# Expert rows weighed on the way out of PSUM and summed in DRAM by an adding scatter

## The chip, the cores and the metric

One core of a Trainium2 chip runs the kernel. The metric is device time in microseconds (us), as the median of several runs of the same program. The kernel before takes 1257.65 us (three runs, 1256.83 to 1258.01). Five engines work beside one another on the core: TensorE (PE, matrix products), VectorE (DVE), ScalarE (ACT), GpSimd (POOL) and SyncE (SP, which only issues transfers). Sixteen DMA engines move data between DRAM and the on-chip memory (SBUF); matrix products land in PSUM, which has eight banks of 128 x 512 fp32.

## The reference, cut to what matters

A transformer-like encoder layer for 1536 tokens of width 1024, in fp32. The first half (adaLN, spatial gating, pooling, output projection, layer norm) is not touched except that some work is put beside it. The second half is a mixture of 32 experts with two experts per token:

```python
g_w  = softmax(g_logits)[g_idx]                       # top-1 group
e_w  = softmax(top2(e_logits in group)) * g_w         # two weights per token
for each block of 128 rows of one expert:             # rows sorted by expert
    xb = h_pad[tok]
    gu = xb @ w_gate_up[e]
    y  = (silu(gu[:, :512]) * gu[:, 512:]) @ w_down[e]
    out[tok] += y * w[:, None]
x = layer_norm(ALPHA * x + g2 * out, ln2_g, ln2_b)
```

So there are 3072 pairs of token and expert. For the last layer norm each token needs the weighted sum of its two expert rows.

## The kernel before, in words

Activations and weights are split into a high and a low fp32r part, and each product is made of three fp32r matmuls (`three`: high by high, high by low, low by high). ACT makes the high parts, DVE the low ones.

**The expert loop.** The router's result is a list of 39 blocks of 128 rows, each of one expert. Block i runs through all engines, each of which has its own in-order queue:

- POOL: `gather(i)` copies the block's column of row numbers into `g_idx` and gathers 128 rows of 4 KB into `xg`; `scatter(i)` copies the column of `table_s` into `s_idx`, waits for `y_ready` and scatters the block's result `y_sb` into `y_rows`. In one pass of POOL's loop `gather(i + 2)` stands ahead of `scatter(i - 1)`. Row numbers past the bound are left out, so that only real rows are written. `y_rows` has 3072 rows, one for each pair.
- PE: `gate_up(i)`, transposes of the next `xg`, `down(i - 1)`, transposes of the activations (`a_transposes_e`).
- ACT (`expert_block`): three high parts of the next expert's gate and up weights (`high_gu`), `silu`, `high_xT`, the fourth `high_gu`, two `high_dn`, `take_y(i - 1)` (copies the result of `down` from PSUM banks 5 and 6 to `y_sb`, L1035), `high_aT(i)` (L1020). The weight work is done only where the expert changes.
- DVE: the low parts in the same order (`low_gu` L1514, `gate` L1524, `low_xT`, `low_dn` L1518, `low_aT` L1528).
- SP: loads of 1 MB each into seven slots for gate and up weights and four for down weights (L611, L619); a load is released when PE has used its slot.

**The end.** SP reads layer-1 rows into `fin` (L674) and the last constants (L682), waits until all scatters have landed, and then reads for each of the 12 token tiles the two rows of each token, `y0` and `y1` (L690, L691). PE forms the weighted sum with matmuls against diagonal matrices of weights (`diag`, L2086 and L2087). The last block is not scattered: its rows are weighed, kept in SBUF (`last_h`, `last_l`) and added by two matmuls with a one-hot matrix (L2090, L2091). To find its rows and weights there is a chain of small DVE and PE operations (L1595 to L1613, L2069, L2072), and `clear_last` writes zeros to its places in `y_rows` early on. Then for each tile DVE multiplies by the gate (L1624, two halves out of PSUM), adds `ALPHA * x` with a row sum (L1628), ACT makes mean and squares (L1114, L1116), POOL the reciprocal deviation (L820, L822), DVE subtracts the mean and multiplies by the gain (L1631) and makes the final scale and bias (L1636). For two of the 12 tiles (`PE_TILES`) the final scale is two matmuls per half on PE (L2097 with the bias row, L2098 with a diagonal of deviations) and ACT copies the result from PSUM (L1108) and stores it.

## Time and profile before

| | before |
|---|---|
| median of three runs | 1257.65 us |
| the profiled execution's own time | 1256.84 us |
| its span (first to last instruction) | 1255.1 us |
| mean granted clock of TensorE | 0.989 |
| busy: PE, DVE, ACT, POOL | 1221.6, 905.0, 614.6, 216.6 us |
| DMA | 329.21 MB, mean 262 GB/s |
| start of the expert loop's first silu | 479.4 us, then 38 equal blocks of 17.68 us but for the first (16.35) |
| last `take_y` of the loop | 1172.71 us |

"Span" is what the trace covers; the device time is 1.7 us more. The table's shares are averages over stages with different limits, so a change is read from its own stage. Times within the trace count from the start of the span. An instruction's row gives its start, how long it took, the engine, the line of the kernel, the operation and the tiles (out<-in); in square brackets stands how long the engine sat idle before it and who ended that.

### The profile page before, as it was taken

To read this page: it belongs to the slowest core of one execution; us is meant where nothing else is said; L and a number is where in the kernel's file an instruction comes from. 1 tells how busy PE (TensorE), PEld (TensorE's weight loads), DVE (VectorE), ACT (ScalarE), POOL (GpSimd) and SP (SyncE) were. 2 spreads that over 40 slices of the span, in tenths; PEclk is the share of its full clock that TensorE was granted. 3 is DMA by queue.
4 is the path that set the end of the run, shared out by engine and by line. 5 is a ranking of instruction groups with operands and counts; after the bars stand their busy time and mean duration, and the time that the engine had idled before them with its cause. 6 is when DMAs were issued, how large, how long until landed. Compare 5 with 4: busy or idle time off the path is not lost.

```text
span 1255.1 us, 25398 instructions
## 1 busy us (share of the span) xinstructions
PE 1221.6 (97%) x7491; PEld 1005.2 (80%) x7492; DVE 905.0 (72%) x1138; ACT 614.6 (49%) x681; POOL 216.6 (17%) x282
## 2 busy tenths in 40 slices
PE   6999999999999998999999999999999999999897
PEld 5889999998888855888888888888888888888553
DVE  3546345657999988856887566745889888998497
ACT  3331111131222244547775565645777877787523
POOL 0042311000111111111121111111121221222122
PEclk8999999999999999999999999999999999999998
DMA  9944311035333588767998766955999999998994
GB/s 312 303 135 133 120 51 35 18 135 184 120 116 128 207 308 305 293 257 283 373 400 348 262 261 246 345 219 214 377 402 403 396 400 397 389 395 305 337 407 170
DMA packets 122711, 329.21 MB, mean 262 GB/s; under 512 B 12888, under 2 KB 44704, under 8 KB 122660
## 3 DMA queue, kind: packets, MB, share of 16 engines
q1 hardware_dynamic: 107700, 288.08, 61.5%
q0 software_dynamic: 13088, 34.13, 7.6%
q10 hardware_dynamic: 1872, 6.29, 1.3%
q8 instruction: 35, 0.57, 0.2%
q14 instruction: 16, 0.13, 0.0%
HBM read 296.97 MB, written 39.39 MB: 268 GB/s over the span
## 4 chain that ended last, share of the span: by engine, by line
PE 79%; DVE 10%; issue 3%; DMA 3%; SPq 2%; POOL 2%; ACT 1%; POOLq 0%; DVEq 0%; ACTq 0%
PE bank L1660 19%; PE bank L1662 19%; PE bank L1661 19%; PE bank L1673 4%; PE bank L1675 4%; PE bank L1674 3%; PE bank L1991 3%; POOL rstd L756 2%; PE bank L2086 1%; PE bank L2087 1%; PE bank L2015 1%; DVE h L1378 1%; DMA sh2b<-mod_rows 1%; PE bank L1720 1%; PE bank L1729 1%
## 5 line engine op out<-in xcount | busy, mean ns | idle before, releaser
L1514 DVE TENSOR_TENSOR gu_l<-gu_raw,gu_h (+1 forms) x128 | 287.3, 2287 | 39.4 <-ACT gu_h L1006 25.4
L1660 PE MATMUL bank<-gu_h,xT_h 128*128 (+1 forms) x624 | 247.2, 396 | 1.8 <-DVE xT_l L1533 1.5
L1006 ACT ACTIVATE gu_h<-gu_raw (+1 forms) x128 | 239.0, 1927 | 9.9 <-issue 7.1
L1662 PE MATMUL bank<-gu_h,xT_l 128*128 (+1 forms) x624 | 243.8, 391 | 0.0
L1661 PE MATMUL bank<-gu_l,xT_h 128*128 (+1 forms) x624 | 243.4, 390 | 0.0
L1518 DVE TENSOR_TENSOR dn_l<-dn_raw,dn_h (+1 forms) x64 | 143.6, 2286 | 7.3 <-ACT dn_h L1010 3.9
L1660 PEld LDWEIGHTS bank<-gu_h,xT_h 128*128 128x128 f32 x624 | 117.6, 188 | 25.3 <-issue 2.2
L1662 PEld LDWEIGHTS bank<-gu_h,xT_l 128*128 128x128 f32 x624 | 117.5, 188 | 25.0
L1661 PEld LDWEIGHTS bank<-gu_l,xT_h 128*128 128x128 f32 x624 | 117.7, 189 | 23.3
L1660 PE MATMUL bank<-dn_h,aT_h 128*128 (+1 forms) x308 | 123.2, 400 | 0.0
L1662 PE MATMUL bank<-dn_h,aT_l 128*128 (+1 forms) x308 | 120.1, 390 | 0.0
L1661 PE MATMUL bank<-dn_l,aT_h 128*128 (+1 forms) x308 | 120.0, 390 | 0.0
L1673 PE MATMUL bank<-hT_h,win_h 128*128 128x256 f32 x384 | 111.3, 290 | 8.3 <-DVE hT_l L1192 7.2
L1010 ACT ACTIVATE dn_h<-dn_raw (+1 forms) x64 | 119.0, 1912 | 0.6 <-issue 0.6
L1675 PE MATMUL bank<-hT_h,win_l 128*128 128x256 f32 x384 | 108.4, 282 | 0.0
L1016 ACT ACTIVATE act_s<-bank 128x512 f32<-128x512 f32 x39 | 23.3, 598 | 173.6 <-PE bank L1662 173.6
L1674 PE MATMUL bank<-hT_l,win_h 128*128 128x256 f32 x384 | 108.3, 282 | 0.0
L793 POOL DMA_INDIRECT y_rows<-y_sb,s_idx x38 | 70.5, 1856 | 186.6 <-ACT y_sb L1035 181.0
L1673 PEld LDWEIGHTS bank<-hT_h,win_h 128*128 128x128 f32 x384 | 73.4, 191 | 10.6 <-DVE hT_l L1192 7.5
L1524 DVE TENSOR_TENSOR act_s<-bank,act_s 128x512 f32<-128x512 f32 x39 | 27.0, 692 | 75.2 <-ACT act_s L1016 75.2
L1660 PE MATMUL bank<-wout_h,z_h 128*128 128x512 f32 x192 | 78.2, 407 | 0.0
L1662 PE MATMUL bank<-wout_h,z_l 128*128 128x512 f32 x192 | 75.9, 395 | 0.0
(312 smaller groups left out, 2037.6 us busy)
## 6 DMA issues: line engine op xcount, KB each, us to landing
gu_raw<-in_w_gate_up SPq DMA_DIRECT2D x128, 1024.0 KB, 8.8
dn_raw<-in_w_down SPq DMA_DIRECT2D x64, 1024.0 KB, 8.2
y<-y_rows SPq DMA_DIRECT2D x22, 512.0 KB, 8.4
ada_raw<-in_w_ada SPq DMA_DIRECT2D x20, 512.0 KB, 7.2
ada_raw<-in_w_ada SPq DMA_DIRECT2D x10, 1024.0 KB, 5.6
win_raw<-in_w_in SPq DMA_DIRECT2D x8, 768.0 KB, 9.0
h_rows<-h SPq DMA_DIRECT2D x12, 512.0 KB, 2.7
fin<-x_rows SPq DMA_DIRECT2D x12, 512.0 KB, 11.3
```

The source lines that it names most:

```text
L793: nc.gpsimd.indirect_dma_start(out=y_d, out_offset=bass.IndirectOffsetOnAxis(ap=s_idx[:, 0:1], axis=0), in_=y_sb[:], in_offset=None, bound ...
L1006: nc.scalar.activation(gu_slot(gu_h, e, c), gu_slot(gu_raw, e, c), ACT.Copy).then_inc(S["gu_split_h"], 1)
L1010: nc.scalar.activation(dn_slot(dn_h, e, c), dn_slot(dn_raw, e, c), ACT.Copy).then_inc(S["dn_split_h"], 1)
L1514: nv.tensor_tensor(gu_slot(gu_l, e, c), gu_slot(gu_raw, e, c), gu_slot(gu_h, e, c).bitcast(F32), ALU.subtract).then_inc(S["gu_split_l"], 1)
L1518: nv.tensor_tensor(dn_slot(dn_l, e, c), dn_slot(dn_raw, e, c), dn_slot(dn_h, e, c).bitcast(F32), ALU.subtract).then_inc(S["dn_split_l"], 1)
L1660: mm(out, lh, rh, start=start, stop=False)
L1661: mm(out, lh, rl, start=False, stop=False)
L1662: return mm(out, ll, rh, start=False, stop=stop)
L1673: mm(out, win_h[:, k, c], hT_h[s][:, k, :], start=start, stop=False)
L1674: mm(out, win_h[:, k, c], hT_l[s][:, k, :], start=False, stop=False)
L1675: return mm(out, win_l[:, k, c], hT_h[s][:, k, :], start=False, stop=stop)
L1991: last = nc.tensor.transpose(ps[2 + k // 4][:, (k % 4) * P:(k % 4 + 1) * P], xg[:, k * P:(k + 1) * P], ident[:])
```

## The change

- **Weights.** The two weights of each token are made in the loop's first block instead of the second, and ACT writes them to DRAM (`w_rows`, 3072 numbers). For each block POOL now gathers its 128 weights into `w_slot`, by indices from `table_s`. `take_y` multiplies by `w_slot` as it copies, so it now waits for that gather, and for the scatter before.
- **Sum.** `y_rows` has one row per token. The scatter adds in DRAM (`compute_op=ALU.add`), by token numbers from a second table, `table_t`. Each scatter waits until the one before has landed. `y_rows` is cleared beforehand by 12 transfers that ACT issues in the mixer stage (`clear_y`).
- **The last block** goes the same way as the others: gather of weights, `take_y`, scatter. The small chains, `diag`, `onehot`, `last_h` and `last_l` and their matmuls are gone.
- **End.** SP loads all 12 `fin` tiles at once, and one `y` tile per token tile. DVE multiplies it by the gate in SBUF in one instruction. Ten tiles instead of two get their final scale on PE.

```diff
-PE_TILES = (NT - 4, NT - 3)
+PE_TILES = tuple(range(NT - 2))
+W_ROWS = T
...
-        y_d = nc.dram_tensor("y_rows", (PAIRS, D), F32).ap()
+        y_d = nc.dram_tensor("y_rows", (T, D), F32).ap()
+        w_d = nc.dram_tensor("w_rows", (2 * W_ROWS, 1), F32).ap()
...
-            for t in range(6):
+            for t in range(NT):
                 load_x1(t)
...
                 if t >= F_SLOTS:
-                    sp.wait_ge(S["y_summed"], 2 * (t - F_SLOTS + 1))
-                for part in ((slice(0, 512), slice(512, D)) if t == 0 else (slice(0, D),)):
-                    sp.dma_start(y0[s][:, part], y_d[bass.ds(t * P, P), part]).then_inc(...)
-                    sp.dma_start(y1[s][:, part], y_d[bass.ds(T + t * P, P), part]).then_inc(...)
+                    sp.wait_ge(S["f_taken"], t - F_SLOTS + 1)
+                sp.dma_start(ys[s][:], y_d[bass.ds(t * P, P), :]).then_inc(y_loaded[s], 16)
...
             def scatter(i):
-                pool.wait_ge(S["y_scattered"], 16 * i + 16)
-                nc.gpsimd.tensor_copy(s_idx[:], table_s[:, bass.ds(column(i), 1)]).then_inc(S["y_idx"], 1)
-                pool.wait_ge(S["y_idx"], i + 1)
+                if not (isinstance(i, int) and i == 0):
+                    pool.wait_ge(S["y_scattered"], 16 * i)
+                col = column(i)
+                nc.gpsimd.tensor_copy(s_idx[:], table_s[:, bass.ds(col, 1)]).then_inc(S["y_idx"], 1)
+                nc.gpsimd.tensor_copy(t_idx[:], table_t[:, bass.ds(col, 1)]).then_inc(S["y_idx"], 1)
+                pool.wait_ge(S["y_idx"], 2 * i + 2)
+                pool.wait_ge(S["y_ready"], i + 1)
+                pool.sem_inc(S["pool_carrier"], 1)
+                nc.gpsimd.indirect_dma_start(out=w_slot[:], out_offset=None, in_=w_d, in_offset=bass.IndirectOffsetOnAxis(ap=s_idx[:, 0:1], axis=0),
+                                             bounds_check=W_ROWS + T - 1, oob_is_err=False).then_inc(S["w_loaded"], 16)
                 pool.wait_ge(S["y_ready"], i + 2)
                 pool.sem_inc(S["pool_carrier"], 1)
-                nc.gpsimd.indirect_dma_start(out=y_d, out_offset=bass.IndirectOffsetOnAxis(ap=s_idx[:, 0:1], axis=0),
-                                             in_=y_sb[:], in_offset=None, bounds_check=PAIRS - 1,
-                                             oob_is_err=False).then_inc(S["y_scattered"], 16)
+                nc.gpsimd.indirect_dma_start(out=y_d, out_offset=bass.IndirectOffsetOnAxis(ap=t_idx[:, 0:1], axis=0),
+                                             in_=y_sb[:], in_offset=None, bounds_check=T - 1,
+                                             oob_is_err=False, compute_op=ALU.add).then_inc(S["y_scattered"], 16)
...
             with pool.Fori(2, n_blocks) as i:
                 gather(i + 2)
                 scatter(i - 1)
-            nc.gpsimd.iota(iota_t[:], pattern=[[1, T]], base=0, channel_multiplier=0, ...)
+            scatter(last_block)
...
+            def clear_y(i):
+                if i == 1:
+                    act.wait_ge(S["lT_zeroed"], 1)
+                for t in range(3 * (i - 1), 3 * i):
+                    nc.scalar.dma_start(y_d[t * P:(t + 1) * P, :].rearrange("p (a n) -> p a n", n=P), lT[:, None, :].to_broadcast([P, D // P, P])).then_inc(S["y_cleared"], 16)
...
             def take_y(i):
                 act.wait_ge(S["dn_used"], 2 * i + 2)
-                act.wait_ge(S["y_scattered"], 16 * i + 16)
+                act.wait_ge(S["w_loaded"], 16 * i + 16)
+                if not (isinstance(i, int) and i == 0):
+                    act.wait_ge(S["y_scattered"], 16 * i)
                 for b in range(2):
-                    last = nc.scalar.activation(y_sb[:, 512 * b:512 * (b + 1)], ps[5 + b][:], ACT.Copy)
+                    last = nc.scalar.activation(y_sb[:, 512 * b:512 * (b + 1)], ps[5 + b][:], ACT.Copy, scale=w_slot[:, 0:1])
                 last.then_inc(S["y_ready"], 1)
...
+                    act.wait_ge(S["tab_ready"], 2)
+                    for c in range(2):
+                        nc.scalar.dma_start(..., out=w_d[c * W_ROWS:c * W_ROWS + T, :].rearrange("(t p) o -> p (t o)", p=P), in_=wts[:, c, :]).then_inc(S["w_stored"], 16)
...
-            act.wait_ge(S["tab_ready"], 3)
-            for t in range(NT):
-                for c in range(2):
-                    last = nc.scalar.activation(diag[:, c, t, :], ident[:], ACT.Copy, scale=wts[:, c, t:t + 1])
...
+            take_y(last_block)
...
             def f_residual(t):
-                for b in range(2):
-                    dve.wait_ge(S["y_summed"], 2 * t + b + 1)
-                    c = slice(512 * b, 512 * (b + 1))
-                    last = nv.tensor_tensor(gated[:, c], ps[bank + b][:], g2b[q][:, c], ALU.mult)
-                last.then_inc(S["f_gated"], 1)
+                q, y = 0 if t < SEQ_TILES[0][1] else 1, ys[t % F_SLOTS]
+                dve.wait_ge(y_loaded[t % F_SLOTS], 16 * (t // F_SLOTS + 1))
+                nv.tensor_tensor(y[:], y[:], g2b[q][:], ALU.mult).then_inc(S["f_gated"], 1)
...
             down_last()
+            down(last_block, NE - 1, (1,))
             pe.wait_ge(S["list_dve"], 5)
-            nc.tensor.transpose(ps[7][:, 0:P], row_sel[:], ident[:]).then_inc(S["list_pe"], 1)
-            down(last_block, NE - 1, (1,))
...
-                    mm(ps[bank + b][:], diag[:, 0, t, :], y0[slot][:, n], start=True, stop=False)
-                    mm(ps[bank + b][:], diag[:, 1, t, :], y1[slot][:, n], start=False, stop=False)
...
             for i, t in enumerate(PE_TILES):
                 pe.wait_ge(S["f_diag"], i + 1)
                 pe.wait_ge(S["f_gained"], t + 1)
+                if i >= F_BANKS:
+                    pe.wait_ge(S["f_copied"], 2 * (i - F_BANKS) + 2)
```

How the instructions stand on POOL, from the end of the loop's body on (L772 and L775 are `gather`, `ISA` rows are register work), before:

```order
82 L772 COPY g_idx<-table_g 128x1
84 L775 DMA xg<-h_rows,g_idx 128x1024
90 L789 COPY s_idx<-table_s 128x1
92 L793 DMA y_rows<-y_sb,s_idx 3072x1024
95 L812 IOTA iota_t 128x1536
```

and now, where L752 and L755 are the same `gather`:

```order
79 L752 COPY g_idx<-table_g 128x1
81 L755 DMA xg<-h_rows,g_idx 128x1024
87 L762 COPY s_idx<-table_s 128x1
89 L763 COPY t_idx<-table_t 128x1
91 L767 DMA w_slot<-w_rows,s_idx 128x1
93 L771 DMA y_rows<-y_sb,t_idx 1536x1024
101 L762 COPY s_idx<-table_s 128x1
103 L763 COPY t_idx<-table_t 128x1
106 L767 DMA w_slot<-w_rows,s_idx 128x1
108 L771 DMA y_rows<-y_sb,t_idx 1536x1024
```

The gather of weights has come between the gather of rows and the scatter, on the same queue, and the whole sequence stands once more behind the loop for the last block.

On DVE, one token tile at the end (of tile 5 and the steps of the tiles before it that run with it), before:

```order
651 L1624 TENSOR_TENSOR gated<-bank,g2b_217 128x512 x2
652 L1628 SCALAR_TENSOR_TENSOR fin_199,f_sum<-fin_199,gated 128x1024
653 L1631 SCALAR_TENSOR_TENSOR fin_198<-fin_198,f_mean,ln_gb 128x1024
654 L1636 SCALAR_TENSOR_TENSOR fin_197<-fin_197,f_rstd,ln_bb 128x1024
```

and now:

```order
627 L1582 TENSOR_TENSOR y_208<-y_208,g2b_214 128x1024
628 L1585 SCALAR_TENSOR_TENSOR fin_200,f_sum<-fin_200,y_208 128x1024
629 L1588 SCALAR_TENSOR_TENSOR fin_199<-fin_199,f_mean,ln_gb 128x1024
```

Three instructions a tile are left of five; the fifth, the final scale, has gone to PE for ten tiles. On PE what stands behind the last down projection was, for one half tile, four matmuls of the sum:

```order
2462 L2086 MATMUL bank<-y_3_209,diag 128x512
2463 L2087 MATMUL bank<-y_3_213,diag 128x512
2464 L2090 MATMUL bank<-last_h,onehot 128x512
2465 L2091 MATMUL bank<-last_l,onehot 128x512
2466 L2097 MATMUL bank<-ln_bb,ones_row 128x512
2467 L2098 MATMUL bank<-fin_202,diag_r 128x512
```

and is now the final scale alone, 20 times two matmuls:

```order
2367 L1619 MATMUL bank<-dn_h,aT_l 128x512
2368 L2034 MATMUL bank<-ln_bb,ones_row 128x512
2369 L2035 MATMUL bank<-fin_196,diag_r 128x512
2370 L2034 MATMUL bank<-ln_bb,ones_row 128x512
2371 L2035 MATMUL bank<-fin_196,diag_r 128x512
```

## Rows read from the trace of the kernel before

**Rows 1.** Windows: stretch, length; busy us of PE, PEld, DVE, ACT, POOL; clock; DMA; GB/s.

```profile
100.00:200.00 100.00, 100.00 (x1173) 92.70 (x1172) 47.63 (x120) 15.76 (x28) 28.28 (x36) 1.00 0.31 96
1000.00:1100.00 100.00, 100.00 (x477) 83.39 (x476) 89.20 (x59) 77.69 (x68) 21.13 (x24) 1.00 1.01 396
```

**Rows 2.** The page: GB/s in 40 slices of 31.4 us.

```profile
GB/s 312 303 135 133 120 51 35 18 135 184 120 116 128 207 308 305 293 257 283 373 400 348 262 261 246 345 219 214 377 402 403 396 400 397 389 395 305 337 407 170
```

**Rows 3.** Timeline of ACT in a block late in the loop, then two blocks on.

```profile
1095.57 0.60 ACT L1016 ACTIVATE act_s<-bank 128x512 f32<-128x512 f32 x1 [3.44 <-PE bank L1662]
1097.42 1.92 ACT L1006 ACTIVATE gu_h<-gu_raw  x1
1102.82 1.09 ACT L1035 ACTIVATE y_sb<-bank 128x512 f32<-128x512 f32 x2
1104.26 5.55 ACT L1006 ACTIVATE gu_h<-gu_raw  x3
1113.25 0.60 ACT L1016 ACTIVATE act_s<-bank 128x512 f32<-128x512 f32 x1 [3.44 <-PE bank L1662]
...
1148.61 0.60 ACT L1016 ACTIVATE act_s<-bank 128x512 f32<-128x512 f32 x1 [3.33 <-PE bank L1662]
...
1150.71 1.92 ACT L1006 ACTIVATE gu_h<-gu_raw  x1
```

**Rows 4.** Timeline of DVE in the same block.

```profile
1101.78 4.49 DVE L1518 TENSOR_TENSOR dn_l<-dn_raw,dn_h  x2
...
1106.79 6.69 DVE L1514 TENSOR_TENSOR gu_l<-gu_raw,gu_h  x3
1113.88 0.69 DVE L1524 TENSOR_TENSOR act_s<-bank,act_s 128x512 f32<-128x512 f32 x1 [0.41 <-ACT act_s L1016]
```

**Rows 5.** Timeline of POOL in the same block.

```profile
1098.27 0.99 POOL L775 DMA_INDIRECT xg<-h_rows,g_idx  x1 [0.83 <-POOL g_idx L772]
1099.26 0.20 POOL L789 COPY s_idx<-table_s 128x1 int32 x1
1104.77 2.36 POOL L793 DMA_INDIRECT y_rows<-y_sb,s_idx  x1 [5.31 <-ACT y_sb L1035]
```

**Rows 6.** Line L793, the scatter: issue to landing.

```profile
DMA to landing us min/median/max: 3.2/8.1/10.8
```

**Rows 7.** DMA queue of POOL: packets, MB, share of 16 engines.

```profile
q0 software_dynamic: 13088, 34.13, 7.6%
```

**Rows 8.** Chain of waits at the end: start, us, what.

```profile
1172.71 0.39 ACT y_sb L1035
...
1175.80 3.99 DMA y_rows<-y_sb,s_idx
1179.80 0.33 SPq L690
```

**Rows 9.** Line L690, the load of y0: issue to landing.

```profile
DMA to landing us min/median/max: 3.0/6.6/9.1
```

**Rows 10.** Timeline of DVE at the end: three starts of the gate.

```profile
1232.65 1.28 DVE L1624 TENSOR_TENSOR gated<-bank,g2b 128x512 f32<-128x512 f32 x2
...
1237.52 1.28 DVE L1624 TENSOR_TENSOR gated<-bank,g2b 128x512 f32<-128x512 f32 x2
...
1241.18 1.28 DVE L1624 TENSOR_TENSOR gated<-bank,g2b 128x512 f32<-128x512 f32 x2
```

**Rows 11.** Timeline of PE at the end: the two tiles scaled there.

```profile
1238.35 1.12 PE L2097 MATMUL bank<-ln_bb,ones_row 1*128 1x512 f32 x2
...
1242.56 1.12 PE L2097 MATMUL bank<-ln_bb,ones_row 1*128 1x512 f32 x2
```

**Rows 12.** Timeline of ACT at the end: squares of the last tile.

```profile
1244.00 1.15 ACT L1116 ACTIVATE squares<-fin,f_mean 128x1024 f32<-128x1024 f32 x1
```

**Rows 13.** Windows, columns as in rows 1: the clock after PE's pauses.

```profile
15.00:20.00 5.00, 3.32 (x14) 3.23 (x15) 2.21 (x4) 3.04 (x6) 0.00 (x0) 0.55 1.11 331
20.00:25.00 5.00, 4.73 (x82) 3.92 (x80) 1.76 (x1) 0.52 (x2) 0.00 (x0) 0.77 1.04 391
...
1248.00:1250.00 2.00, 0.00 (x0) 0.00 (x0) 1.37 (x2) 0.00 (x0) 0.00 (x0) 0.50 0.85 342
```

More of the change, by code:

```diff
@@ L337, in encoder @@
             assert r.at == at + 24 * KB
[L338 to L343 removed]
+        ys = [Region(W0 + 4 * s * KB).take(f"y_{s}", [P, D]) for s in range(F_SLOTS)]
+        r = Region(W0 + 8 * GU_SLOTS * KB + 4 * KB)
         squares = r.take("squares", [P, D])
@@ L1574, in expert_block @@
                     low_gu(e_next, 3)
-                if second:
+                if first:
                     weights()
-                if first:
                     for c in range(2):
```

112 lines of the change are left out of this document (19 added, 93 removed).

## The prediction, made before the changed kernel ran

> **What bounds the kernel now.** I read the windows first. In the mixer stage PE is busy all the time and the DMA engines a third of it; in the late expert loop PE is busy all the time too, at full clock, and beside it the DMA engines stand at a share of 1.01 and 396 GB/s [rows 1]. The page's slices show that this is no single spot: from the 29th to the 36th, 8 slices of 31.4 us = 251 us or 14 blocks of 17.68 us, they read 377 to 403 GB/s [rows 2]. So PE sets the pace of the loop, and DMA is right behind it. How near, ACT tells: the fourth high part of a block needs a 1 MB load that has just come, and starts 1.85 us after the silu in one block (1095.57 to 1097.42) and 2.10 us three blocks on (1148.61 to 1150.71) [rows 3]. The loads slip slowly against PE already. Between them ACT sits idle 3.44 us a block, ahead of the silu, and DVE 0.41 us ahead of the gate [rows 3, 4]. That idle time is all the give there is.
>
> Behind the loop the chain of waits goes from `take_y` (1172.71) to the scatter (issued 1175.80, landed 3.99 later) to SP's loads of y (1179.80) [rows 8], and then with DVE: a tile takes 1237.52 - 1232.65 = 4.87 us there, and 1241.18 - 1237.52 = 3.66 us where the final scale is left to PE [rows 10].
>
> **The end, step by step.** All times count from the start of the span.
>
> (a) `take_y` of the block before the last now waits for its weights. Their gather is issued behind the gather of rows: that one starts 1098.27 in rows 5 when the silu is at 1095.57, the copy of indices follows, one more copy of 0.20 and the pause of 0.83 that stands ahead of an indirect transfer come on top, so it starts some 4.9 us after the silu [rows 3, 5]. Such a block's silu is at 1166.3 (1148.61 + 17.68), which gives 1171.2. From issue to landing the nearest rows are the scatter's: 3.2 at least, 8.1 in the median, 10.8 at most [rows 6]; it could also be under 3.2, since 512 bytes are moved rather than 512 KB. In the same moments SP now has twelve `fin` loads of 512 KB in flight instead of six, and the rows' gather stands ahead in the same queue. I take 7 us, between the least and the median but nearer the latter: 1178.2, that is 5.5 us later than `take_y` starts today. Ends: 1.7 and 9.3 us. Everything behind follows, the last down projection too, since `high_aT` stands behind `take_y` on ACT.
> By the Trainium skill (DMA: Bandwidth & Descriptors, "Anatomy of one DMA — SWDGE (gpsimd) path") a transfer from POOL takes 2.0 us plus its bytes at 436 GB/s. With it the wait would be 0.5 us instead of 5.5. No row here shows a transfer so small that far ahead of its queue, so it is no term of my sum.
>
> (b) `take_y` 1.1 us [rows 3], then the scatter: 1175.80 is 2.0 us after 1173.8, the end of today's `take_y` [rows 3, 8]. It starts at 1181.3. It lands 4.0 us later when it only writes [rows 8]; adding needs the old row as well, and I give it 1 us more (0 to 4): 1186.3.
>
> (c) Only then does POOL copy the last block's indices and gather its weights: two copies of 0.20 and the pause of 0.83 [rows 5], then 3.2 us, the least landing [rows 6], as traffic is over by then: 1190.7. PE's last down projection is done by then. `take_y` 1.1, the step to the scatter 2.0, landing 5.0: 1198.8. Before, this whole second round did not exist, because the last block stayed in SBUF.
>
> (d) SP issues, and the first y tile lands after 3.0 us, the least landing of such a load [rows 9]: DVE starts at 1202.1.
>
> (e) DVE needs per tile 3.6 to 3.66 us [rows 10]: its gate out of SBUF lies between half of a 2048-wide one (6.69 / 3 / 2 = 1.1 us, rows 4) and the two halves of today (1.28). But PE needs more: the two tiles that it scales today start 4.21 us apart, back to back (1238.35 and 1242.56) [rows 11]. Ten tiles make 42.1 us, and PE is the slowest of the three. It starts when tile 0's diagonal is made, which on ACT stands behind tile 1's squares: four DVE instructions of about 1.2 us, then 2 us of ACT: 7.0 us after DVE. By then PE has done nothing for some 20 us. Its clock is at 0.50, that is at 1.2 GHz, already 2 us after PE has stopped at the end, and after the pause at the start it was 0.55 for 5 us and 0.77 for another 5 [rows 13]. The clock lost there is 0.45 x 5 + 0.23 x 5 = 3.4 us, and as PE is the slowest, it is all paid. ACT's last squares come after the copies of tile 8: 7.0 + 9 x 4.21 + 3.4 + 1.3 = 49.6 us after DVE's start, and from their start to the span's end there are 1255.1 - 1244.0 = 11.1 us today [rows 12]. The span would end at 1202.1 + 60.7 = 1262.8: **7.7 us later** than today. The saving of DVE's 4.87 us per tile, of 24 diagonals on ACT and of half of the y traffic is real, but it is spent on the second round of (c), on (a) and on a PE at 4.21 us.
>
> **The loop.** (f) The adding scatter reads each row that it adds to. POOL's queue carries 34.13 MB at 7.6% of the span [rows 7]; 41 gathers of 0.52 MB are 21.5 of it, so the scatters are 12.6 MB. At 7.6% x 1255 / 34.13 = 2.8 us per MB a second reading costs 35 us of all DMA engines, 0.9 us per block. The gather of weights, 128 packets, I put at 0.1: 1.0 us per block, bounds 0 (where the reading hides under the other direction's traffic) and 2.7 (three times the plain price). In the 14 saturated blocks the loads come 14 us later in all. ACT takes up 3.44 of idle, and as PE has the down projection between a silu and the next `gate_up`, I give as much again to that: about 7 us pass before PE waits. Left are **7 to 8 us**; with 0.9 x 14 - 7 = 5.6 and with 2.7 x 14 - 7 = 31 at the upper end, 0 at the lower.
> The Trainium skill (Collectives: The Full Stack, "The bandwidth ceiling: the fold count and why AG ≠ RS ≠ AR") says that it is not the adding that costs in a DMA engine but the second source, both being read through one ring, at half the rate. By that rule the second reading can't hide, and rival 1 below falls away; the plain scatters of rows 6 and 7 can't tell.
>
> (g) `take_y` waits for weights in every block. They are issued 4.9 us after the silu and needed at 7.25 (1102.82 - 1095.57) [rows 3]. With (a)'s landing they come 3 to 5 us late. ACT then finishes its three high parts (5.55 us) at about its silu, where it now has 3.44 us [rows 3]; DVE, with 4.49 us of low parts ahead of `low_aT` [rows 4], loses about 2 us and goes on. PE needs neither before the next block but one. Cost 0, cover: those 3.44 us. It is used up if the weights land later than some 12 us after the silu.
>
> (h) Clearing: 6.3 MB in 12 transfers beside a mixer stage with a DMA share of 0.31 and ACT busy 15.76 of 100 us [rows 1]: 0. The weights made one block earlier and stored as 4-byte pieces in a busy queue: 0, at most 3.
>
> Sum: 1255.1 + 7.7 + 8 = 1270.8 of span. The profiled execution took 1.7 us more than its span, and the median of the runs lies 0.8 above that execution: 1273.
>
> **Rivals.**
> 1. *The reading for the sum hides* in the loop: (f) is 0, only the end costs, 1257.65 + 7.7 = 1265. For it: a plain scatter reads SBUF and writes DRAM, so DRAM's side could have room. Against it: a share of 1.01.
> 2. *The recurrence of weights and scatter takes over the loop.* `take_y`, scatter, its landing, the next gather of weights, its landing, the next `take_y`: 1.1 + 0.9 + 8.1 + 1.2 + 3.2 to 8.1 = 14.5 to 19.4 us, against 17.68 [rows 3, 5, 6]. With the landing 1 to 2 us longer for the adding it is over 17.68 in saturated blocks, by 1 to 2 us in each of 14 to 20: 1257.65 + 7.7 + 25 = 1290.
> 3. *The end gains* (the other side): weights are 512 bytes and land ahead of `take_y`, adding costs nothing, and PE's clock holds. Then DVE starts at 1172.7 + 1.1 + 2.0 + 4.0 + 1.2 + 3.2 + 1.1 + 2.0 + 4.0 + 3.3 = 1194.6 and the end comes 57.3 later, at 1251.9: 1254.5, faster by 0.25%. The point from which it decides is (a): each microsecond for which `take_y` waits is lost, and at a wait of 1 us with the rest as here there is no change.
> 4. *Weights cheap but clock cold*: 3 without the clock: 1258, no change.
>
> **How the numbers follow.** Forecast, 0.42: 1273 (own range 1264 to 1283). Rival 1: 0.20. Rival 2: 0.22. Rival 3: 0.08. Rival 4: 0.08. About 0.2% (2.5 us) is what a measurement can tell from no change. Faster 0.09 (rival 3 and a little), same 0.09, slower 0.82. The range runs from 1258 to 1296: it leaves out rival 3 and the far half of rival 2.
>
> **What would show it.** Right: ACT idle ahead of `take_y` in the loop with the gather of weights as releaser; the fourth high part waiting for its load in the late blocks, PE idle there ahead of `gate_up`; landings of the scatter over 8.1 us in the median; two scatters one after the other before the first load of y; L2034 starts 4.21 us apart per two pairs, later ones evenly, the first at a clock near 0.5. Wrong: blocks of 17.68 us to the end with 400 GB/s and no wait of PE, or `take_y` within 1 us of its place today, or DVE without idle time between the tiles of the end.

## The result, and the profile after

| | before | after |
|---|---|---|
| median, runs on the same chip | 1256.83 us (5 runs) | 1393.38 us (5 runs, 1389.23 to 1395.73) |
| ratio, 95% interval | 1 | 1.1081 (1.1065 to 1.1096) |
| span of the profiled execution | 1255.1 us | 1387.5 us |
| up to the first silu of the expert loop | 495.8 us | 495.0 us |
| first to last silu (38 intervals) | 670.5 us | 760.3 us |
| last silu to DVE's first tile of the end | 20.5 us | 38.6 us |
| from there to the end of the span | 68.4 us | 93.6 us |

The change made the kernel 10.8% slower, and the time is far outside the range of the prediction (1258 to 1296). The four stages of the table are cut at an instruction of ACT or DVE that both kernels have. Of the 132.4 us that the span grew, 89.8 are in the loop, 18.1 between the loop and the end's first tile, 25.2 in the end, and -0.8 ahead of the loop.

A correction to the table that stands ahead of the prediction: it puts the first silu of the loop at 479.4 us. It starts at 495.78, and the 39th at 1166.29; the 38 intervals between them are 16.35 and 37 times 17.68. The prediction used the 17.68 and not the start, so none of its numbers hangs on it.

The waits of the changed kernel (engine, line and what it writes, releaser: us in total, times, longest) name the largest item:

```profile
ACT y_sb L1025 <- DMA w_slot<-w_rows,s_idx: 254.5, 39, 10.9
POOL y_rows L771 <- ACT y_sb L1025: 214.9, 38, 7.4
DVE aT_l L1512 <- ACT aT_h L1008: 164.8, 32, 8.7
```

`take_y` waits for its 128 weights in every one of the 39 blocks, 6.5 us on average, and DVE then waits for ACT. Issue to landing of the gather of weights (L767), least, median, most:

```profile
DMA to landing us min/median/max: 2.3/5.5/7.6
```

ACT in a late block, where [rows 3] shows 3.44 us of idle time, ahead of the silu:

```profile
1087.71 1.92 ACT L998 ACTIVATE dn_h<-dn_raw  x1
1100.54 1.27 ACT L1025 ACTIVATE y_sb<-bank,w_slot 128x512 f32<-128x512 f32 x2 [10.92 <-DMA w_slot<-w_rows,s_idx]
1101.70 0.60 ACT L1008 ACTIVATE aT_h<-bank 128x512 fp32r<-128x512 f32 x1
1102.31 5.51 ACT L994 ACTIVATE gu_h<-gu_raw  x3
1107.73 0.58 ACT L1004 ACTIVATE act_s<-bank 128x512 f32<-128x512 f32 x1
...
1117.72 1.27 ACT L1025 ACTIVATE y_sb<-bank,w_slot 128x512 f32<-128x512 f32 x2 [3.03 <-DMA w_slot<-w_rows,s_idx]
```

The idle time has gone to `take_y`; the silu follows the high parts with no gap (5.51 us from 1102.31, silu at 1107.73). So it is late because ACT is late, and no longer because PE is. POOL in the same block, against [rows 5]:

```profile
1093.19 2.19 POOL L767 DMA_INDIRECT w_slot<-w_rows,s_idx  x1 [0.88 <-POOL t_idx L763]
1102.69 1.60 POOL L771 DMA_INDIRECT y_rows<-y_sb,t_idx  x1 [7.31 <-ACT y_sb L1025]
1103.74 0.75 POOL L752 COPY g_idx<-table_g 128x1 int32 x1
1105.29 2.34 POOL L755 DMA_INDIRECT xg<-h_rows,g_idx  x1 [0.80 <-POOL g_idx L752]
1108.86 2.33 POOL L762 COPY s_idx<-table_s 128x1 int32 x1 [1.23 <-DMA y_rows<-y_sb,t_idx]
1111.14 0.17 POOL L763 COPY t_idx<-table_t 128x1 int32 x1
1112.20 1.03 POOL L767 DMA_INDIRECT w_slot<-w_rows,s_idx  x1 [0.88 <-POOL t_idx L763]
```

This is a circle: `take_y` 1100.54, scatter 1102.69, landed 1108.86, copies of indices, gather of weights 1112.20, landed and `take_y` 1117.72. It takes 17.2 us here, nearly as long as a block of PE's (17.68), and nothing in it overlaps. It is one of the short rounds: from one `take_y` to the next the 38 rounds take 12.6 to 25.3 us, 19.5 on average. The next round takes 22.95, and in it POOL waits for something else:

```profile
1119.87 1.61 POOL L771 DMA_INDIRECT y_rows<-y_sb,t_idx  x1 [6.65 <-ACT y_sb L1025]
1129.91 0.18 POOL L752 COPY g_idx<-table_g 128x1 int32 x1 [8.43 <-PE bank L1948]
1133.09 2.33 POOL L767 DMA_INDIRECT w_slot<-w_rows,s_idx  x1 [0.88 <-POOL t_idx L763]
```

The gather of rows stands ahead of the gather of weights on POOL, and it may not overwrite `xg` before PE has transposed the rows in it (L1948). So in such a round the circle runs through PE: `take_y`, the operands that ACT and DVE make behind it, PE, the gather of rows, the gather of weights. Of POOL's waits between a scatter and the next gather of weights, this is the larger part:

```profile
POOL g_idx L752 <- PE bank L1948: 162.5, 31, 14.4
POOL s_idx L762 <- DMA y_rows<-y_sb,t_idx: 30.0, 16, 5.2
```

Two of these 31 waits (12.06 and 14.44 us) lie ahead of the first scatter. Copies that took 0.20 us in [rows 5] take up to 2.33, and the issue of a gather 2.34 in place of 0.99.

What the loop lost is not all idle time of PE. First to last silu, before and then after:

```profile
495.80:1166.30 670.50, 668.40 (x3169) 556.55 (x3168) 509.17 (x345) 452.42 (x410) 124.15 (x152) 1.00 0.87 333
495.00:1255.30 760.30, 698.60 (x3170) 571.17 (x3169) 506.45 (x346) 458.32 (x410) 278.57 (x224) 0.96 0.85 297
```

PE was idle for 61.7 us in place of 2.1, and for the same matmuls it was busy 30.2 us longer, at a granted clock of 0.96 in place of 1.00. In e2 and e7, where the circle is broken, the clock is 1.00 and 0.99 and PE is busy 672.9 and 674.5 us: the slower clock came with the waits and went with them.

At the start of the loop POOL stands still for another reason, the stores of the weights as 4-byte pieces:

```profile
513.95 0.96 POOL L755 DMA_INDIRECT xg<-h_rows,g_idx  x1 [0.79 <-POOL g_idx L752]
535.90 0.18 POOL L762 COPY s_idx<-table_s 128x1 int32 x1 [20.98 <-DMA w_rows<-wts]
```

ACT issued these stores from 502.15 on (2.10 us for two); they had landed at 535.9. The first three intervals of the loop take 22.62, 24.80 and 21.94 us, 17.7 more than in the kernel before.

The end: ACT, then windows (columns as in [rows 1]).

```profile
1255.29 0.60 ACT L1004 ACTIVATE act_s<-bank 128x512 f32<-128x512 f32 x1 [9.76 <-PE bank L1619]
...
1269.10 1.27 ACT L1025 ACTIVATE y_sb<-bank,w_slot 128x512 f32<-128x512 f32 x2 [8.11 <-DMA w_slot<-w_rows,s_idx]
1270.26 0.60 ACT L1008 ACTIVATE aT_h<-bank 128x512 fp32r<-128x512 f32 x1
1281.73 1.27 ACT L1025 ACTIVATE y_sb<-bank,w_slot 128x512 f32<-128x512 f32 x2 [10.88 <-DMA w_slot<-w_rows,s_idx]
```

```profile
1310.00:1330.00 20.00, 20.00 (x21) 5.00 (x20) 9.69 (x10) 8.20 (x17) 7.63 (x6) 0.50 0.47 158
1350.00:1370.00 20.00, 20.00 (x21) 4.99 (x20) 8.83 (x10) 8.20 (x17) 7.21 (x6) 0.50 0.20 79
```

Two rounds of gather and scatter stand one after the other, as forecast. But then PE is busy for all of 20 us and its granted clock stays at 0.50, that is 1.2 GHz where 1.00 is 2.4 GHz, to the end. The bias matmuls of two tiles start 8.01 us apart (1304.95, 1312.96, 1320.97 for every second one), in place of the 4.21 of [rows 11].

### The profile page after: what moved, and what is told of

Read it like the earlier page. It is cut to its first block, busy times and chain, and to the rows that moved or that the text cites. A ratio compares the mean times of both kernels' runs of the same rounds, so it can differ in the third digit from the quotient of the medians.

```text
span 1387.5 us, 25445 instructions
## 1 busy us (share of the span) xinstructions
PE 1269.5 (91%) x7408; PEld 1009.3 (73%) x7409; DVE 886.7 (64%) x1105; ACT 625.9 (45%) x681; POOL 390.2 (28%) x359
## 3 DMA queue, kind: packets, MB, share of 16 engines
q0 software_dynamic: 14336, 34.16, 10.0%
## 4 chain that ended last, share of the span: by engine, by line
PE 53%; DMA 15%; DVE 11%; issue 10%; POOL 4%; ACT 3%; SPq 1%; POOLq 1%; ACTq 1%; DVEq 1%
PE bank L1617 11%; PE bank L1618 10%; PE bank L1619 10%; DMA w_slot<-w_rows,s_idx 7%; DMA y_rows<-y_sb,t_idx 4%; PE bank L1630 3%; PE bank L1632 3%; PE bank L1631 3%; PE bank L2035 3%; PE bank L2034 3%; DMA w_rows<-wts 2%; PE bank L1948 2%; ACT gu_h L994 1%; POOL rstd L736 1%; DVE gu_l L1498 1%
## 5 line engine op out<-in xcount | busy, mean ns | idle before, releaser
L1617 PE MATMUL bank<-gu_h,xT_h 128*128 (+1 forms) x624 | 254.8, 408 | 31.7 <-issue 30.2
L1619 PE MATMUL bank<-gu_h,xT_l 128*128 (+1 forms) x624 | 250.5, 401 | 0.0
L1618 PE MATMUL bank<-gu_l,xT_h 128*128 (+1 forms) x624 | 250.0, 401 | 0.0
L1617 PEld LDWEIGHTS bank<-gu_h,xT_h 128*128 128x128 f32 x624 | 121.9, 195 | 62.2 <-issue 37.4
L1025 ACT ACTIVATE y_sb<-bank,w_slot 128x512 f32<-128x512 f32 x78 | 49.4, 685 | 254.5 <-DMA w_slot<-w_rows,s_idx 254.5
L1619 PEld LDWEIGHTS bank<-gu_h,xT_l 128*128 128x128 f32 x624 | 121.4, 194 | 26.6
L1618 PEld LDWEIGHTS bank<-gu_l,xT_h 128*128 128x128 f32 x624 | 121.9, 195 | 25.0
L1512 DVE TENSOR_TENSOR aT_l<-bank,aT_h 128x512 fp32r<-128x512 f32 x39 | 26.9, 690 | 164.9 <-ACT aT_h L1008 164.8
L771 POOL DMA_INDIRECT y_rows<-y_sb,t_idx x39 | 64.6, 1657 | 222.4 <-ACT y_sb L1025 214.9
L752 POOL COPY g_idx<-table_g 128x1 int32 (+1 forms) x41 | 32.5, 793 | 185.3 <-PE bank L1948 162.5
L767 POOL DMA_INDIRECT w_slot<-w_rows,s_idx x39 | 68.7, 1762 | 35.7 <-POOL t_idx L763 32.8
```

Of the source, the lines that this page charges most:

```text
L767: nc.gpsimd.indirect_dma_start(out=w_slot[:], out_offset=None, in_=w_d, in_offset=bass.IndirectOffsetOnAxis(ap=s_idx[:, 0:1], axis=0), bou ...
L771: nc.gpsimd.indirect_dma_start(out=y_d, out_offset=bass.IndirectOffsetOnAxis(ap=t_idx[:, 0:1], axis=0), in_=y_sb[:], in_offset=None, bound ...
L1617: mm(out, lh, rh, start=start, stop=False)
L1618: mm(out, lh, rl, start=False, stop=False)
L1619: return mm(out, ll, rh, start=False, stop=stop)
```

## The experiments

Each kernel's profile is cut at the same places. All rows are from one profiled execution each. "First three" is what the first three intervals take beyond those of before.

| kernel | median us | ratio to before, interval | loop | first three | last silu to DVE | DVE to end |
|---|---|---|---|---|---|---|
| before | 1256.8 | 1 | 670.5 | 0 | 20.5 | 68.4 |
| after | 1393.4 | 1.1081 (1.1065, 1.1096) | 760.3 | 17.7 | 38.6 | 93.6 |
| e1 plain scatter | 1369.0 | 1.0881 (1.0850, 1.0913) | 744.8 | 19.8 | 34.7 | 93.6 |
| e2 no gather of weights | 1312.6 | 1.0433 (1.0403, 1.0464) | 689.7 | 8.3 | 32.5 | 93.6 |
| e3 PE warmed | 1388.8 | 1.1039 (1.0955, 1.1122) | 767.6 | 21.9 | 39.4 | 88.6 |
| e4 whole stores | 1374.4 | 1.0925 (1.0822, 1.1028) | 739.3 | 4.1 | 39.6 | 93.6 |
| e5 full rows in place of bias | 1341.2 | 1.0681 (1.0652, 1.0710) | 756.5 | 12.9 | 39.7 | 50.7 |
| e6 two tiles on PE | 1360.6 | 1.0835 (1.0810, 1.0860) | 757.0 | 14.3 | 39.9 | 66.6 |
| e7 weights a block ahead | 1321.2 | 1.0521 (1.0496, 1.0546) | 696.5 | 15.4 | 34.8 | 93.6 |
| e8 = e7 + whole stores + two tiles | 1279.8 | 1.0189 (1.0169, 1.0209) | 681.2 | 0.5 | 34.2 | 67.3 |
| e9 = e8 + ten tiles, full-row bias | 1263.2 | 1.0048 (1.0033, 1.0063) | 681.0 | 0.5 | 34.8 | 50.7 |
| e10 = e9 + plain scatter | 1246.9 | 0.9917 (0.9899, 0.9936) | 671.0 | 0.4 | 29.0 | 49.7 |
| e11 = e9 + shorter last rounds | 1257.2 | 1.0001 (0.9992, 1.0010) | 681.1 | 0.6 | 28.4 | 50.0 |
| e12 = e11 + padding left out | 1255.4 | 0.9992 (0.9980, 1.0005) | 680.5 | 0.9 | 26.6 | 50.4 |

The medians of e1 to e7 are of two runs each. The loop of the change stands as it was in e3, e5 and e6 too; it took 767.6, 756.5 and 757.0 us there, 760.3 in the change. So a single loop time of this kind is good to some 11 us, and differences below that say nothing. The kernels without the circle repeat better (e8, e9 and e11: 681.2, 681.0 and 681.1).

**e1, the scatter only writes.** The sum over a token's experts is left out.

```diff
-  oob_is_err=False, compute_op=ALU.add).then_inc(S["y_scattered"], 16)
+  oob_is_err=False).then_inc(S["y_scattered"], 16)
```

> The changed kernel whose scatter only writes and does not add (a token's second row replaces the first; the sum is left out). First to last silu took 760.3 us in the changed kernel, 670.5 before. Theory R (take_y waits in every block for a gather of weights that stands behind the last scatter's landing): the round keeps nearly its length, landings of the scatter shorten by 1 to 2 us, the loop falls to 725 to 750. Theory D (the DMA engines are over full with the second reading of the sum): the loop falls to about 690, what is left being the slow start of the first three blocks.

Total 24.4 us less, 15.5 of the span's 18.9 in the loop. The adding has a price, but most of the loop's loss stands without it. Inside the circle its price can't be told from that of the longer circle; e10 does that. That a shorter landing helps so little fits the rows of POOL above: it waits more for PE than for the landing.

**e2, no gather of weights.** `w_slot` is set to 1 once; the weights are left out of the output.

```diff
-  nc.gpsimd.indirect_dma_start(out=w_slot[:], ..., in_=w_d, ...).then_inc(S["w_loaded"], 16)
-  act.wait_ge(S["w_loaded"], 16 * i + 16)
+  act.wait_ge(S["w_loaded"], 1)
```

> The changed kernel without the gather of weights and without the wait for it: every row is weighed by 1, index copies and the adding scatter stay. Theory R: ACT finds its operands ready, PE sets the pace of 17.68 us again and the loop from first to last silu falls to 671 to 690 (the first blocks' slow start from the store of weights may stay in part). Theory D: the adding scatter is still there, so the loop stays above 730. A third, S: the start alone (first three intervals 22.6, 24.8, 21.9 us) would stay at +18.

The loop falls from 760.3 to 689.7 us, and from its sixth to its 29th interval a block takes 17.68 again. So 70.6 of the 89.8 us hang on this gather or on the wait for it; e7 parts the two. The slow start stays in part, 8.3 us.

**e3, PE warmed ahead of the end.** 64 matmuls of 128x512 ahead of the tiles' scale.

```diff
+  pe.wait_ge(S["y_ready"], last_block + 2)
+  for _ in range(64):
+      mm(ps[7][:], aT_h[:, 0, :], dn_slot(dn_h, NE - 1, 1)[:, 0, 0:512], start=True, stop=True)
```

> The changed kernel with 64 matmuls of 128x512 on PE (result unused) between the last take_y and the first token tile. Theory C (PE comes out of its pause at the lower clock and the pattern of its final scales never lets it rise, while the same pattern keeps the higher clock once it has it): the clock is 1.00 in the last stage, a tile takes 4.21 us on PE instead of 8.01, and the stage from DVE's first tile to the end takes 55 to 58 us instead of 93.6: 36 to 38 us less in all. Rival (the matmul with one row of weights, or fp32 operands, is slow whatever went before): the clock falls back to 0.50 within the stage and less than 10 us are gained.

Windows of this kernel:

```profile
1300.00:1310.00 10.00, 10.00 (x45) 8.05 (x44) 7.25 (x9) 3.29 (x7) 3.01 (x3) 1.00 0.86 306
1310.00:1320.00 10.00, 10.00 (x16) 2.51 (x15) 9.93 (x12) 5.03 (x11) 5.80 (x5) 0.77 0.55 179
1320.00:1340.00 20.00, 20.00 (x21) 4.99 (x20) 9.86 (x12) 8.19 (x17) 5.97 (x5) 0.50 0.49 177
```

The clock is 1.00 when the scale begins, and falls back to 0.50 under it, with PE busy all the time. A cold start is not the cause; something in these matmuls is. The end is only 5.0 us shorter, and the total can't be told from that of the change: theory C fell.

**e4, weights stored in whole pieces.** Each partition's 12 weights as one piece of 48 bytes; the indices are not adapted, so tokens get each other's weights.

```diff
-  w_d[...].rearrange("(t p) o -> p (t o)", p=P)
+  w_d[...].rearrange("(p t) o -> p (t o)", p=P)
```

> The changed kernel whose two stores of the weights write 48 bytes in a piece (256 pieces) instead of 4 (3072 pieces); the order in DRAM differs, so rows are weighed by other tokens' weights. If the 3072 pieces are what delays the loads and the first scatter (their landing took 32.5 us), the first three blocks go back from 22.6, 24.8, 21.9 to some 17 to 18 us each and the total falls by 14 to 18 us. If the first take_y is late for the ordinary gather of weights, under 5 us are gained.

The first three intervals lose only 4.1 us in place of 17.7. The page gives 5.0 us from the stores' issue to landing. The circle goes on after that: 739.3. The third interval is 21.63 us still, so the return to 17 or 18 that was expected came in two of the three. The total fell by 19.0 us, from two runs that lie 10.8 apart.

**e5, matmuls with all rows in place of the bias.** Same number and width, but each sums over 128 rows (K is 128) and not over one (K is 1). The output is twice the scaled value without `ln2_b`.

```diff
-  mm(out, ones_row[:], ln2_b[0:1, n], start=True, stop=False)
+  mm(out, diag_r[:, i, :], fin[t][:, n], start=True, stop=False)
```

> The 20 bias matmuls of the end, which have one partition as K (ones_row by a row of ln2_b), are replaced by as many with all 128 partitions (the diagonal by fin once more); the output is then twice the scaled value and lacks ln2_b. Number and width of the matmuls stay. Theory K (matmuls with one row keep PE at its lower clock, though it is busy 20.00 of 20.00 us): the granted clock rises to 1.00 within the first tiles, a tile then takes 4.21 us and not 8.01, and the stage from DVE's first y tile to the end shrinks from 93.6 to 60 to 68 us; total about 1365. Rival M (the clock stays at 0.50 for this fp32 work whatever K is, or for the small waits between the pairs): the stage stays at 93.6, the clock at 0.50, the total at 1389 to 1396.

```profile
1290.00:1300.00 10.00, 2.32 (x3) 1.18 (x4) 9.29 (x11) 4.11 (x9) 4.54 (x4) 0.50 0.68 239
1300.00:1320.00 20.00, 20.00 (x44) 8.71 (x43) 19.42 (x23) 14.49 (x31) 10.85 (x10) 0.92 0.75 251
```

From the same cold start (0.50) the clock now rises, and the end takes 50.7 us in place of 93.6: 42.9 us for the shape of 20 matmuls. That is less than the 60 to 68 expected, and 17.7 less than before the change.

**e6, two tiles on PE.**

```diff
-PE_TILES = tuple(range(NT - 2))
+PE_TILES = (NT - 4, NT - 3)
```

> Only the part of the change that gives ten tiles' final scale to TensorE is undone: two tiles stay on it, as before. Theory P (PE at 8.01 us a tile and 0.50 of its clock paces the end): the stage from DVE's first y tile to the end falls from 93.6 to 60 to 66 us (ten tiles at 4.87 us on DVE, two at 3.66, and the last stretch), total 1393 - 30 = 1360 to 1366. Rival Q (ACT, POOL or the loads of y would pace it at nearly the same length): 80 us or more, total over 1378. The loop and its first blocks stay as they are.

66.6 us from DVE's first tile to the end, at the upper edge of what theory P has, far from the 80 of rival Q. So the move of eight more tiles to PE, which was to relieve DVE, cost 27.0 us by itself.

**e7, weights gathered a block ahead.**

```diff
+  nc.gpsimd.tensor_copy(w_now[:], w_slot[:])       # when take_y(i - 1) is done
+  nc.gpsimd.tensor_copy(s_idx[:], table_s[:, bass.ds(column(i + 1), 1)])
+  gather_w()                                        # the weights of block i + 1
-  ... ACT.Copy, scale=w_slot[:, 0:1])
+  ... ACT.Copy, scale=w_now[:, 0:1])
```

> The weights of a block are gathered one block earlier, into w_slot; POOL copies them to a second column w_now when take_y of the block before is done, and take_y scales by that. Gather, adding scatter, the 4-byte stores and the end stay. Theory R (take_y's wait for the weights closes a circle with the scatter and slows the loop): the loop takes 685 to 705 us in place of 760.3, nearly the 689.7 of the run without that gather, ACT no longer waits for w_slot (254.5 us in 39 waits after the change), the total is 1325 to 1345. Rival T (the gather's own traffic and POOL's time for it slow the loop): 740 or more, total over 1370. In addition the last two rounds lose one landing of the weights, about 5 us.

The gather is still made and 696.5 us are left of 760.3, with the blocks at 17.68 from the fourth to the 28th interval. It was the wait and not the traffic. The total, 1321.2, lies a little under the 1325 to 1345 expected.

**e8, the three mended.** e7, the stores of e4 with indices to match, two tiles on PE.

```diff
+  step(nv.tensor_scalar(table_s[:], table_t[:], P - 1, None, ALU.bitwise_and))
+  step(nv.scalar_tensor_tensor(tab_neg[:], table_s[:], NT - 1.0 / P, tab_neg[:], ALU.mult, ALU.add))
```

> Everything that the runs so far name is mended together, and the idea of the change stays: weights gathered one block ahead, stored as 48-byte pieces of a partition (the scatter table's indices follow that order), two tiles' final scale on TensorE. If the three causes (the weights' wait, the 4-byte stores, PE at 0.50 at the end) are all there is besides the adding, then loop 680 to 692, from the last silu to DVE's first tile 27 to 33, from there to the end 60 to 66: span 495 + 686 + 30 + 63 = 1274, total 1268 to 1284, still 1 to 2% slower than before: what is left is the adding scatter (some 10 to 20 us in the loop) and the second round at the end (some 10 us). Rival: one of them returns when another is gone (the DMA queues stay saturated): over 1300.

1279.8, as forecast, and none of the causes came back. The parts lie less well: the two stages behind the loop were to take 27 to 33 and 60 to 66 us and took 34.2 and 67.3. One by one the three mends gave 72.2, 19.0 and 32.8 us, 124.0 together; at once they give 113.6, so they overlap in part. Its loop is 15.3 us shorter than e7's, and 14.9 of these are in the first three intervals.

**e9, ten tiles on PE, bias by full rows.**

```diff
-  ones_row = r.take("ones_row", [1, P])
+  ones_row = r.take("ones_row", [P, P])             # ones in row 0, zeros below
-  mm(out, ones_row[:], ln2_b[0:1, n], start=True, stop=False)
+  mm(out, ones_row[:], ln2_b[:, n], start=True, stop=False)
```

> The mended kernel (weights one block ahead, 48-byte stores), but with ten tiles' scale on TensorE again as in the change, and the bias by 128 rows: the left side is a 128 by 128 matrix with ones in its first row and zeros below, the right side the copy of ln2_b that all partitions hold. Theory K (only the one-row matmuls held the clock down): the stage from DVE's first y tile to the end takes 50 to 53 us, as in the run with the doubled diagonal (50.7), in place of 67.3 with two tiles; granted clock 1.00 within two tiles; total 1280 - 16 = 1262 to 1266, within 1% of before. Rival Z (it is the products that count, and a matrix that is zero in 127 rows is as bad as one row): clock 0.50, the stage 93.6, total 1306.

Windows, then PE's bias matmuls of one and a half tiles:

```profile
1210.00:1220.00 10.00, 1.21 (x2) 0.72 (x3) 8.17 (x9) 3.29 (x7) 3.93 (x4) 0.50 0.76 278
1220.00:1230.00 10.00, 10.00 (x19) 4.19 (x19) 9.62 (x12) 6.09 (x14) 5.07 (x5) 0.79 0.59 204
1230.00:1240.00 10.00, 10.00 (x25) 4.38 (x24) 9.90 (x13) 8.18 (x18) 6.15 (x7) 1.00 0.79 274
```

```profile
1231.84 1.02 PE L2052 MATMUL bank<-ln_bb,ones_row 128*128 128x512 f32 x2
1233.55 1.02 PE L2052 MATMUL bank<-ln_bb,ones_row 128*128 128x512 f32 x2
1235.27 1.02 PE L2052 MATMUL bank<-ln_bb,ones_row 128*128 128x512 f32 x2
```

A left side that is zero below its first row serves as well as the doubled diagonal of e5. At the clock of 1.00 a tile now takes 3.43 us (1231.84 to 1235.27), where a tile with the one-row bias took 4.21 at the same clock [rows 11].

**e10, e9 with a plain scatter** (the edit of e1; the sum is left out).

> The kernel with the full-row bias, but the scatter writes and does not add (the sum over a token's experts is left out: its last writer stays). Theory A (the adding reads each row once more and that costs only where the DMA engines are full): the loop falls from about 681 to 671 to 674 us, its last ten blocks back to 17.68, and the two landings at the end shrink by 1 us each; total 11 to 13 us less than with adding. Rival G (it is the gather of weights or the late loads that fill the DMA engines there): the loop stays at 678 or more, total within 5 us.

All intervals from the fourth on are 17.68 again; the gain is 10.0 us in the loop, 5.8 ahead of the end and 1.0 in it, of 17.2 in the span. The median fell by 16.3 us, more than the 11 to 13 expected: ahead of the end 5.8 came in place of 2, which was not followed up. In the late stretch 990 to 1176 us of e9, ACT's fourth high part waits for its load:

```profile
ACT gu_h L1007 <- DMA gu_raw<-in_w_gate_up: 45.1, 10, 5.5
```

Without the adding this wait is gone. In the same stretch, the loads of gate and up weights (KB each, median us to landing), first with adding, then without:

```profile
gu_raw<-in_w_gate_up SPq DMA_DIRECT2D x34, 1024.0 KB, 15.5
```

```profile
gu_raw<-in_w_gate_up SPq DMA_DIRECT2D x34, 1024.0 KB, 9.3
```

And the queue of POOL over the whole span, columns as in [rows 7], with adding and without:

```profile
q0 software_dynamic: 14336, 34.16, 10.7%
```

```profile
q0 software_dynamic: 14336, 34.16, 7.7%
```

The same bytes are counted, but the packets take 10.7% of 1262.4 us = 135.1 in place of 7.7% of 1245.2 = 95.9: 39.2 us, 1.0 us for each of the 39 scatters.

**e11, a shorter way through the last two blocks.**

```diff
+  y_sb2 = r.take("y_sb2", [P, D])
...                                                  # POOL: w_now and gather_w ahead of the wait for the landing
-  take_y(last_block)
+  take_y(last_block, y_sb2)                         # waits for no landing
-  for t in range(NT): load_x1(t)
+  for t in range(6): load_x1(t)                     # the other six between the loads of y
```

> The kernel with the full-row bias and a shorter way through the last two blocks: POOL hands over the weights ahead of its wait for the landing of the scatter before, the last block goes to an y_sb of its own so that its take_y waits for no landing, and only six x1 rows are loaded during the loop, the other six between the loads of y (as before the change). Theory S (the chain take_y, scatter, landing, scatter, landing is what is between the last silu and DVE's first tile): 34.2 us become 26 to 30, the rest stays, total 4 to 8 us less than with the full-row bias alone: 1255 to 1260, about that of before. Rival L (landings stretch by what traffic is left, or the late x1 loads delay y): within 2 us.

34.8 us become 28.4, as theory S has it; 1257.2 us are the time of before. These are three changes at once, and what each of them gave was not tried.

**e12, padding rows not gathered.**

```diff
-  nc.gpsimd.indirect_dma_start(out=xg[:], ..., in_=h2_d, in_offset=...)
+  nc.gpsimd.indirect_dma_start(out=xg[:], ..., in_=h2_d, in_offset=...,
+                               bounds_check=T, oob_is_err=False)
```

> The best version so far, and from block 4 on the gather of rows of h leaves out a block's padding rows (39 blocks of 128 rows for 3072 pairs: 1920 of 4992 rows are padding); they keep what stood in xg, and their results are dropped by the scatter as before. The last block has indices of its own, made while the landing is awaited. Theory D (the last ten blocks wait because the DMA engines are full, and bytes are what fills them): 38% of 0.52 MB, 0.2 MB or about 0.5 us per saturated block, is given back, nearly half of what the adding costs: the loop falls from 681.1 to 674 to 677 us; the last two blocks gain 1.2 us more from the indices; total 1250 to 1253, 0.3 to 0.5% faster than before. Rival E (it is not the bytes but the adding scatter's way through the queues): loop at 680 or more, total 1255 to 1257.

Theory D fell. POOL's queue moves 26.10 MB in place of 34.16, the DMA share between 1000 and 1080 us is 0.98 in place of 1.02, and the loop takes 680.5 us, not 674 to 677:

```profile
1000.00:1080.00 80.00, 77.44 (x365) 63.94 (x364) 67.68 (x44) 61.43 (x54) 34.26 (x30) 1.00 0.98 366
```

The last rounds gain 1.8 us, 1.2 of them forecast from the indices. No version that makes the whole sum beats the kernel before by more than can be measured; e10, 0.8% faster, leaves the sum out.

## Why the prediction was wrong, step by step

**(g) is the step that failed first.** It had the weights 3 to 5 us late in every block and cost 0, covered by ACT's 3.44 us, and it named the point at which that cover is gone: a landing more than 12 us after the silu. In the block shown `take_y` starts 10 us after the silu (1107.73 to 1117.72), but that silu itself came late, behind the 10.92 us of the wait before. What (g) left out is that cover is spent on a wait only once. The weights wait for the landing of the scatter, which waits for `take_y`, so a delay is not absorbed but handed to the next block. (g) also let PE need none of this before the next block but one; but PE's down projection in the next block needs `low_aT`, which stands behind `take_y`, and PE stood 2.16 us for it in the block shown:

```profile
1103.31 0.79 PE L1617 MATMUL bank<-dn_h,aT_h 128*128 x1 [2.16 <-DVE aT_l L1512]
```

Rival 2 had the circle of scatter and weights, with 14.5 to 19.4 us for it; the round in the rows takes 17.2, the mean of all is 19.5. What rival 2 lacked is the other way round, through PE's transposes and the gather of rows that stands first on POOL, and the clock that falls with PE's waits. Its price was wrong with that: 25 us, 1 to 2 us in 14 to 20 saturated blocks. e7 says 63.8 us in the loop, e2 70.6. How they divide between the two ways round was not tried (a gather of weights ahead of that of the rows would tell); both pass through the wait that e7 takes away. The circle decides outside the saturated blocks too (18.18 to 24.18 us from the fifth interval to the 12th), and where it does ACT's high parts of the next expert stand behind the waiting `take_y`: a block then takes up to 25.06 us. So rival 2 counted too few blocks, and it priced a circle that left out what else stands on its way.

**(e) is the term of the sum that was mis-sized most.** It let PE's clock come back after 3.4 us of loss, by analogy with the pause at the start [rows 13]. The end took 93.6 us in place of 60.7, that is 32.9 more. The other terms were right: PE began 7.1 us after DVE (forecast 7.0), and with nine times 8.01 for nine times 4.21 and no 3.4, the same sum gives 91.5. With a cold start and other matmuls it does come back (e5, e9), and with a warm start and these matmuls it goes (e3). So neither the pause nor the fp32 diagonal is to blame, only the one-row bias. Before the change the same pattern ran for two tiles behind the sums, and the clock was still 1.00 when it ended:

```profile
1242.50:1246.80 4.30, 4.30 (x9) 1.18 (x8) 4.26 (x5) 2.52 (x5) 1.39 (x2) 1.00 0.31 124
```

So [rows 11] was the right row for a tile and the wrong one for ten. The engine named as the bound was right (8.01 us a tile against DVE's 3.66). Full rows, which the sum did not consider, make a tile 3.43 us, less than DVE needs, and the end 50.7.

**(h) was too low.** "At most 3" for the 4-byte stores; the first three intervals lost 17.7 us (12.9 to 21.9 in the other kernels that kept these stores and the wait for the weights), and 13.6 of them go with whole pieces (e4). The 21.0 us that e4 gives in the whole loop are not all the stores': the rest, 7.4, lies in blocks that the circle sets, and is less than these loops differ among themselves. Clearing cost nothing, as forecast: between 100 and 200 us PE is busy 100.00, and the loop begins at 495.0 us, before at 495.8.

**(f) was about right where it can be seen alone.** The forecast was 0.9 us of all DMA engines per scatter and 7 to 8 us for the loop, in the saturated blocks; e10 against e9 shows 1.0 and 10.0, and the way that it takes is the one forecast, a fourth high part that waits for its load. The rule of the Trainium skill (Collectives: The Full Stack, "The bandwidth ceiling: the fold count and why AG ≠ RS ≠ AR"), that a second source is read through the same ring, agrees with these rows: the adding did not hide, rival 1 fell. Its factor of a half can't be told from them, as the queue's time holds the gathers too. The mechanism behind those 10 us is open: 8.06 MB less in the gathers (e12) gave nothing back (0.6 us), so fewer bytes alone do not mend it. The loads of 1 MB land later beside an adding scatter (15.5 us against 9.3), which is shown; whether they queue behind it or share something else was not tried.

**(a) to (d) came out near, (a) partly by luck.** `take_y` of the block before the last comes 13.8 us after the silu (1255.29 to 1269.10), forecast 11.9. But the gather of its weights starts 9.5 us after the silu and not 4.9, as POOL had waited for PE's transposes and its copies took 1.42 and 2.25 us, and then it lands in 4.3 us and not in 7: two errors that nearly cancel. From the last silu to DVE's first tile there are 38.6 us, forecast 35.8. The Trainium skill (DMA: Bandwidth & Descriptors, "Anatomy of one DMA — SWDGE (gpsimd) path") gives 2.0 us and the bytes for such a transfer: the least row, 2.3, agrees, the median of 5.5 in busy queues does not. In (a) the 4.3 us lie between that figure and the 7 taken from the scatter's rows; in (c), with little traffic left, the landing took 2.4, forecast 3.2.

**Rivals 3 and 4** had the end gain, or break even. From the last silu to the end of the span the kernel before takes 88.8 us, the change 132.2. With the full-row bias and the weights a block ahead it is 85.5 (e9), a gain of 3.4 us, near that of rival 3; the conditions that rival 3 names did not hold in the change itself.

## What to carry to other kernels

When a new wait closes a circle of transfers (result, scatter, landing, next operand, next result), idle time beside it is no cover for more than one round: price it in every block, with all that stands ahead of its steps in an in-order queue (here a gather that waits for PE), or fetch the operand a round ahead, which here gave back 63.8 us for one more copy a block. Before work is moved to TensorE, try that very mix of matmuls and read its granted clock, not its busy share: a bias by one row made ten tiles cost 42.9 us more than the same matmuls with 128 rows. For small strided stores count the pieces and not only the bytes: 3072 pieces of 4 bytes cost 13.6 us more at the start of this loop than 256 pieces of 48.

## What the runs showed of the hardware

- Matmuls of one row, half of those in a stretch in which PE was busy 20.00 of 20.00 us, kept the granted clock at 0.50 and brought it down from 1.00 to 0.50 (e3). With 128 rows, 127 of them zero, it was 0.79 and then 1.00 in the same place (e9).
- At a clock of 1.00 a tile of four fp32 matmuls of 512 columns took 4.21 us where two of them had one row, and 3.43 us where all had 128.
- Two stores of 1536 weights each in 4-byte pieces took ACT's queue 2.10 us to issue and had landed 33.7 us after that began; as pieces of 48 bytes they had landed 5.9 us after (e4).
- An adding scatter of 128 rows of 4 KB took 1.0 us more of all 16 DMA engines than a plain one and landed later. Issue to landing in e9, then in e10:

```profile
DMA to landing us min/median/max: 4.5/9.9/11.2
```

```profile
DMA to landing us min/median/max: 3.2/7.6/9.6
```

- Where PE had to wait in the loop of the change, its granted clock was 0.96 on average over the loop, in place of 1.00, and the same matmuls took 30.2 us longer.
- POOL's copies of one column took 0.17 to 2.33 us in the loop of the change, its issues of indirect gathers 0.96 to 2.62.
